# Stick-breaking attention on one core: TensorE turns the logarithm of the weights, ScalarE exponentiates out of PSUM

## The chip, the cores and the metric

One core of a Trainium2 chip runs the whole program. The metric is the device time of one execution in microseconds (us). The kernel before took 1975.42 us, the median of 3 runs (1974.12 to 1976.77).

## The reference

One inference step of a decoder layer: RMSNorm and one wide projection; dilated attention of 12 heads and stick-breaking attention of 8 heads, for 1024 prompt tokens and 8 sampled tokens; sigmoid gates and output projections; a hierarchical mixture of 32 experts; a gated per-layer embedding; a last RMSNorm. The change lies in the stick-breaking attention of the prompt:

```python
z = einsum('bqhd,bkhd->bhqk', q, k) * hd ** -0.5 + bias
log_1mb = where(causal, -softplus(z), 0.0)
suffix  = cumsum(log_1mb, axis=3, reverse=True)
log_a   = -softplus(-z) + suffix - log_1mb
a = where(causal, exp(log_a), 0.0)
out = einsum('bhqk,bkhd->bqhd', a, v)
```

## The kernel before

The program is a row of stages, each written as one instruction list for each engine. The stage of the change is `stick_and_gates`. It does two things side by side: the stick-breaking attention of the prompt, and 10 chunks of the gate projection, whose 344-column matmuls (L666) are dealt out evenly over the steps of the attention, about 11 for each step.

The attention works on 64 units. A unit is one head and one block of 128 queries; heads come in 4 pairs (a pass each), and the 8 query blocks of a pass come in the order 7, 0, 6, 1, 5, 2, 4, 3, so a unit is 8, 1, 7, 2, 6, 3, 5 or 4 tiles of 128 keys wide. Both heads of a block share a pair of steps, an even one and an odd one. Position 0 is the block of 8 tiles, position 1 that of one tile, and so on.

Each engine runs through the same steps s, and each kind of work lags by a fixed number of steps. In step s:

- TensorE issues the scores of both heads, half a block (up to 512 keys) for each step (L630); in odd steps the products with the values (`values`, L650) of the pair whose turning ended in step s-1; half of the step's gate matmuls; the turning of unit s-5 (`turn`, L638: a 128x128 transpose for each tile, in groups of up to four tiles, one PSUM bank for each group, two banks in turn); the other half of the gate matmuls.
- ScalarE first casts a gate weight where one is due (L688) and, in even steps, copies out a finished output block (L709), then scales the scores out of PSUM into z (L718), computes exp(-|z|) and ln(1 + that) of unit s-2 in w (L724, L726), the exponential of unit s-4 in place in z (L731, "RISE"), and copies finished gate sums out of PSUM (L697).
- VectorE adds the causal mask for unit s-1 (L763), runs the reversed running sum for unit s-3 (L769, a scan), splits |z| and max(z, 0) for unit s-1 (L777, L779), subtracts the sum from z for unit s-3 (L784: the logarithm of the weights), and last copies the turned tiles of unit s-5 from PSUM to aT (L791).

`values` waits for `tp_read`, which is counted up by each of those copies: in an odd step it needs the copies of the step before. `turn` waits for the exponential (`a_full`) and for the earlier reader of its PSUM bank (`tp_read`). The lags are set in one line:

```python
FOLD, EXP, SCAN, RISE, TURN, VALUES, EVICT = 1, 2, 3, 4, 5, 6, 7
```

Queues are in order: an engine that waits holds up all that stands behind in its own list. The score bank S of each head is single; z has seven slots, w three, aT two (one for each head).

Of the kernel before, what the change touches and what calls it, by code (L numbers as in the profile page):

```python
# [16 lines left out]
ACT = mybir.ActivationFunctionType  # L17
AX = mybir.AxisListType.X

P = 128  # L20
# [40 lines left out]
def need(eng, sem, value):  # L61

    if not isinstance(value, int) or value > 0:
        eng.wait_ge(sem, value)
# [386 lines left out]
def turn_groups(n):  # L451

    return [(a, min(4, n - a)) for a in range(0, n, 4)]
# [41 lines left out]
def stick_and_gates(nc, g, c0):  # L495
# [5 lines left out]
    with ctx:  # L501
# [5 lines left out]
        STEPS = PAIRS * QT  # L507
        U = 2 * STEPS
        ZB, WB, HALF = 7, 3, 512
        FOLD, EXP, SCAN, RISE, TURN, VALUES, EVICT = 1, 2, 3, 4, 5, 6, 7  # L510
        LAST = U + EVICT
        CH = 2 * KD - c0
        M = KD * 3
# [17 lines left out]
        O = [ps(f"s_O{j}", [P, 512]) for j in range(2)]  # L531
        acc = [ps(f"s_g_acc{j}", [P, 512]) for j in range(2)]
        const, kept = sem("s_const"), g["kept"]
        s_full, z_full, masked, r_full, w_full, e_full, t_full, cum_full, al_full, a_full = map(sem, (
            "s_s_full", "s_z_full", "s_masked", "s_r_full", "s_w_full", "s_e_full", "s_t_full",
            "s_cum_full", "s_al_full", "s_a_full"))
        tp_full, tp_read, o_full, o_read = map(sem, ("s_tp_full", "s_tp_read", "s_o_full", "s_o_read"))
        qkv_in = g["opening"]["qkv_in"]
        gw_in = g["opening"]["gw_in"]
# [8 lines left out]
        def unit(u):  # L548

            st = u // 2  # L550
            return st // QT, u % 2, ORDER[st % QT]
# [15 lines left out]
        def live(s, lag):  # L567

            return 0 <= s - lag < U
# [50 lines left out]
        @block.tensor  # L620
        def _(pe):
            def scores(st, c):
                p_, i = st // QT, ORDER[st % QT]
                x, n = p_ % 2, piece(st, c)
                if st % QT == 0:
                    pe.wait_ge(qkv_in[x], 64 * (p_ // 2 + 1))
                for b in range(2):
                    h = slice(b * HD, (b + 1) * HD)
                    need(pe, z_full, z_first[st, c] - 1 + b)
                    pe.matmul(S[:, b, 0:n], q[x][h, i * P:(i + 1) * P], k[x][h, c * HALF:c * HALF + n],  # L630
                              start=True, stop=True).then_inc(s_full, 1)

            def turn(u):
                pe.wait_ge(a_full, u + 1)
                for n, (t0, m) in enumerate(turn_groups(unit(u)[2] + 1)):
                    need(pe, tp_read, first[u] + n - 1)
                    for t in range(m):
                        last = pe.transpose(tp[(first[u] + n) % 2][:, t * P:(t + 1) * P],  # L638
                                            z[:, u % ZB, (t0 + t) * P:(t0 + t + 1) * P], ident[:, :])
                    last.then_inc(tp_full, 1)  # L640

            def values(st):
                p_, i = st // QT, ORDER[st % QT]
                u = 2 * st + 1
                pe.wait_ge(tp_read, first[u] + count[u])
                need(pe, o_read, st - 1)
                for t in range(i + 1):
                    for b in range(2):
                        h = slice(b * HD, (b + 1) * HD)
                        last = pe.matmul(O[st % 2][h, 0:P], v[p_ % 2][:, t, h], aT[:, b, t * P:(t + 1) * P],  # L650
                                         start=(t == 0), stop=(t == i), skip_group_check=True)
                last.then_inc(o_full, 1)

            def gates(m0, m1):

                for m in range(m0, m1):
                    grp, x = divmod(m, M)
                    c, s = divmod(grp, NSPLIT)
                    t = slice(s * NS, (s + 1) * NS)
                    if x == 0:  # L660
                        pe.wait_ge(gwl_full, c + 1)
                        need(pe, gate_full, grp - 1)
                    kk, part = divmod(x, 3)
                    lhs = (gwl, gwh, gwh)[part]
                    rhs = (uh, ul, uh)[part]
                    last = pe.matmul(acc[grp % 2][:, 0:NS], lhs[:, c % 2, kk, :], rhs[:, kk, t], start=(x == 0),  # L666
                                     stop=(x == M - 1), skip_group_check=True)
                    if x == M - 1:
                        last.then_inc(acc_full, 1)

            for s in range(LAST + 1):
                if s < U and piece(s // 2, s % 2) > 0:
                    scores(s // 2, s % 2)
                if live(s, VALUES) and (s - VALUES) % 2:
                    values((s - VALUES) // 2)
                if s < LAST:
                    gates(fills[s], half(s))
                if live(s, TURN):
                    turn(s - TURN)
                if s < LAST:  # L680
                    gates(half(s), fills[s + 1])

        @block.scalar
        def _(act):
            def cut(c):
                act.wait_ge(gw_in, 16 * (c + 1))
                need(act, acc_full, (c - 1) * NSPLIT)
                act.activation(gwh[:, c % 2, :, :], gw[:, :, :], ACT.Copy).then_inc(gwh_full, 1)  # L688

            def evict(grp):  # L690
                c, s = divmod(grp, NSPLIT)
                if s == 0 and c < 2:
                    act.wait_ge(g["decode_out"][c], 16 * ((c0 + 1 - c) // 2))
                if s == 0:
                    need(act, g_out[c % 2], 16 * (c // 2))
                act.wait_ge(acc_full, grp + 1)
                act.activation(gate[:, c % 2, s * NS:(s + 1) * NS], acc[grp % 2][:, 0:NS], ACT.Copy).then_inc(gate_full, 1)  # L697

            cut(0)
            act.preload_act_table_set("natural_log_exp_and_others")  # L700
            for s in range(LAST + 1):
                for c in range(1, CH):
                    if cut_at[c] == s:
                        cut(c)
                if live(s, EVICT) and (s - EVICT) % 2:
                    st = (s - EVICT) // 2
                    p_, i = st // QT, ORDER[st % QT]
                    act.wait_ge(o_full, st + 1)
                    act.activation(obT[:, p_, i * P:(i + 1) * P], O[st % 2][:, 0:P], ACT.Copy).then_inc(o_read, 1)  # L709
                if s < U and piece(s // 2, s % 2) > 0:  # L710
                    st, c = divmod(s, 2)
                    n = piece(st, c)
                    for b in range(2):
                        u = 2 * st + b
                        act.wait_ge(s_full, z_first[st, c] + b + 1)
                        if c == 0 and u >= ZB:
                            act.wait_ge(tp_full, first[u - ZB] + count[u - ZB])
                        act.activation(z[:, u % ZB, c * HALF:c * HALF + n], S[:, b, 0:n], ACT.Identity, scale=SCALE,  # L718
                                       bias=bias[st // QT % 2][:, b:b + 1]).then_inc(z_full, 1)
                if live(s, EXP):  # L720
                    u = s - EXP
                    n = (unit(u)[2] + 1) * P
                    act.wait_ge(w_full, u + 1)
                    act.activation(w[:, u % WB, 0:n], w[:, u % WB, 0:n], ACT.Exp, scale=-1.0).then_inc(e_full, 1)  # L724
                    act.wait_ge(e_full, u + 1)
                    act.activation(w[:, u % WB, 0:n], w[:, u % WB, 0:n], ACT.Ln, bias=1.0).then_inc(t_full, 1)  # L726
                if live(s, RISE):
                    u = s - RISE
                    n = (unit(u)[2] + 1) * P
                    act.wait_ge(al_full, u + 1)  # L730
                    act.activation(z[:, u % ZB, 0:n], z[:, u % ZB, 0:n], ACT.Exp).then_inc(a_full, 1)  # L731
                for grp in range(CH * NSPLIT):
                    if evict_at[grp] == s:
                        evict(grp)
# [11 lines left out]
        def _(dve):  # L746
# [5 lines left out]
            for s in range(LAST + 1):  # L752
# [27 lines left out]
                if live(s, SCAN):  # L780
# [2 lines left out]
                    dve.wait_ge(cum_full, u + 1)  # L783
                    dve.tensor_tensor(z[:, u % ZB, 0:n], z[:, u % ZB, 0:n], w[:, u % WB, 0:n],  # L784
                                      ALU.subtract).then_inc(al_full, 1)
                if live(s, TURN):
                    u = s - TURN
                    need(dve, o_full, u // 2)
                    for n, (t0, m) in enumerate(turn_groups(unit(u)[2] + 1)):
                        dve.wait_ge(tp_full, first[u] + n + 1)  # L790
                        dve.tensor_copy(aT[:, u % 2, t0 * P:(t0 + m) * P],  # L791
                                        tp[(first[u] + n) % 2][:, 0:m * P]).then_inc(tp_read, 1)


def dilated(nc, g):
# [2196 lines left out]
```

## Time and profile before

| what | value |
|---|---|
| median of 3 runs | 1975.42 us |
| profiled execution, span | 1976.0 us |
| stage of the change, about | 508 to 797 us of the span |
| TensorE / VectorE / ScalarE busy over the span | 88% / 61% / 49% |

The page gives for each engine its busy time over the whole span; a stage has to be read by itself. For that there are views of a stretch: busy time of each engine in a window with the granted TensorE clock (1.00 is 2.4 GHz, 0.50 is 1.2 GHz, values between are means), waits by who waited for whom, groups of instructions by line, and instructions in order of time. A matmul's row shows its latency, so rows of following matmuls overlap; the busy time of a window is their union.

### The profile page before, as it was taken

The numbers are of one execution on the slowest core, as the hardware profiler recorded it, in microseconds if no ns is written. First come the engines' busy times: TensorE is split into PE (matmuls) and PEld (weight loads), VectorE is DVE, ScalarE is ACT, GpSimd is POOL, SyncE is SP. The second block draws the span as 40 slices with busy tenths as digits, with TensorE's granted clock in tenths as the row PEclk, the third lists the DMA queues.
The fourth block names the chain that finished last, engine by engine and source line by source line (L and its number), as shares of the span: only waits on it lengthen the run. The fifth ranks groups of instructions, "written<-read, shape, count | busy, mean of one in ns | idle before, by whom it ended". The sixth has DMA issues, their size and how long they took to land. (4 is left out here: it accounts for less than half of the span.)

```text
span 1976.0 us, 27569 instructions
## 1 busy us (share of the span) xinstructions
PE 1747.3 (88%) x9832; PEld 1483.3 (75%) x9832; DVE 1199.8 (61%) x1550; ACT 976.7 (49%) x1392; POOL 213.4 (11%) x316
## 2 busy tenths in 40 slices
PE   5999999989888888798549967999999999997497
PEld 4999999978666666576548845788888888885485
DVE  6111222153589998442473355899999999996485
ACT  4121111111476776155342014778777877785255
POOL 1000111120000000300130012111111111110100
PEclk8999999989999999899779978999999999999699
DMA  5343455453351200612454316999999999994641
GB/s 170 107 135 110 128 177 159 126 193 118 102 183 54 76 22 23 203 50 76 170 200 153 118 66 238 390 372 379 372 383 379 372 382 381 384 370 189 225 150 66
DMA packets 156394, 392.77 MB, mean 199 GB/s; under 512 B 21923, under 2 KB 95251, under 8 KB 135828
## 3 DMA queue, kind: packets, MB, share of 16 engines
q1 hardware_dynamic: 120676, 320.28, 45.4%
q0 software_dynamic: 15424, 36.00, 5.7%
q10 hardware_dynamic: 20208, 35.35, 5.0%
q8 instruction: 54, 0.88, 0.2%
q14 instruction: 32, 0.26, 0.0%
HBM read 335.32 MB, written 80.58 MB: 210 GB/s over the span
## 5 line engine op out<-in xcount | busy, mean ns | idle before, releaser
L97 PE MATMUL p_acc<-uh,p_wl 128*128 128x344 f32 x720 | 234.3, 325 | 9.6 <-DVE ul L415 9.6
L98 PE MATMUL p_acc<-ul,p_wh 128*128 128x344 f32 x720 | 230.7, 320 | 0.0
L99 PE MATMUL p_acc<-uh,p_wh 128*128 128x344 f32 x720 | 230.5, 320 | 0.0
L392 ACT ACTIVATE p_zc<-p_acc 128x344 f32<-128x344 f32 x90 | 41.2, 458 | 290.2 <-PE p_acc L99 286.4
L2543 DVE TENSOR_TENSOR x_wgl<-x_wg,x_wgh 128x2048 fp32r<-128x2048 f32 x66 | 148.3, 2288 | 36.1 <-ACT x_wgh L2480 20.0
L2543 DVE TENSOR_TENSOR x_wul<-x_wu,x_wuh 128x2048 fp32r<-128x2048 f32 x66 | 148.3, 2289 | 18.7 <-ACT x_wuh L2480 18.7
L2565 DVE TENSOR_TENSOR x_wdl<-u,x_wdh 128x1024 fp32r<-128x1024 f32 x128 | 148.2, 1220 | 10.3 <-ACT x_wdh L2486 10.3
L97 PEld LDWEIGHTS p_acc<-uh,p_wl 128*128 128x128 f32 x720 | 135.9, 189 | 13.1 <-issue 8.6
L428 DVE COPY u<-p_tp 128x512 f32<-128x512 f32 x40 | 25.8, 686 | 185.2 <-PE p_tp L345 185.1
L98 PEld LDWEIGHTS p_acc<-ul,p_wh 128*128 128x128 f32 x720 | 136.0, 189 | 0.0
L99 PEld LDWEIGHTS p_acc<-uh,p_wh 128*128 128x128 f32 x720 | 135.8, 189 | 0.0
L2486 ACT ACTIVATE x_wdh<-u 128x1024 fp32r<-128x1024 f32 x128 | 124.8, 1059 | 0.0
L2480 ACT ACTIVATE x_wgh<-x_wg 128x2048 fp32r<-128x2048 f32 x64 | 119.0, 1915 | 0.0
L2480 ACT ACTIVATE x_wuh<-x_wu 128x2048 fp32r<-128x2048 f32 x64 | 118.6, 1906 | 0.0
L97 PE MATMUL x_G<-x_wgh,x_xl 128*128 128x512 f32 x256 | 102.9, 402 | 6.1 <-DVE x_xl L2537 6.1
L97 PE MATMUL x_Y<-x_wdh,x_hl 128*128 128x512 f32 x256 | 103.6, 405 | 3.8 <-DVE x_hl L2560 3.8
L97 PE MATMUL x_U<-x_wuh,x_xl 128*128 128x512 f32 x256 | 103.4, 404 | 0.0
L99 PE MATMUL x_G<-x_wgh,x_xh 128*128 128x512 f32 x256 | 102.8, 401 | 0.0
L98 PE MATMUL x_G<-x_wgl,x_xh 128*128 128x512 f32 x256 | 102.3, 400 | 0.0
L99 PE MATMUL x_U<-x_wuh,x_xh 128*128 128x512 f32 x256 | 101.2, 395 | 0.0
L98 PE MATMUL x_U<-x_wul,x_xh 128*128 128x512 f32 x256 | 101.0, 394 | 0.0
L99 PE MATMUL x_Y<-x_wdh,x_hh 128*128 128x512 f32 x256 | 100.8, 394 | 0.0
(383 smaller groups left out, 4269.7 us busy)
## 6 DMA issues: line engine op xcount, KB each, us to landing
x_wg<-in_w_gate SPq DMA_DIRECT2D x64, 1024.0 KB
x_wu<-in_w_up SPq DMA_DIRECT2D x64, 1024.0 KB, 7.7
u<-in_w_down SPq DMA_DIRECT2D x32, 2048.0 KB, 12.2
zT<-p_zc ACTq DMA_DIRECT2D x30, 516.0 KB, 3.5
p_w<-in_w_in SPq DMA_DIRECT2D x30, 512.0 KB, 5.5
ztok<-u POOLq DMA_DIRECT2D x20, 512.0 KB, 4.6
m_gate<-gT SPq DMA_DIRECT2D x16, 516.0 KB, 4.4
f_y<-ys POOLq DMA_DIRECT2D x16, 512.0 KB, 5.1
```

Source lines behind the costliest of these rows:

```text
L97: pe.matmul(out, w_low, m_high, start=first, stop=False)
L98: pe.matmul(out, w_high, m_low, start=False, stop=False)
L99: return pe.matmul(out, w_high, m_high, start=False, stop=last)
L392: act.activation(zc[:, b, s * NS:(s + 1) * NS], acc[b * NSPLIT + s][:, 0:NS], ACT.Copy).then_inc(zc_full, 1)
L428: dve.tensor_copy(zk[:, b, t0:t0 + m, :], tp[n][:, :, :]).then_inc(zk_full, 1)
L2480: act.activation(wh[:, HALVES[half], :], w[:, HALVES[half], :], ACT.Copy).then_inc(full, 1)
L2486: act.activation(wdh[:, k, :], wd[:, b, k, :], ACT.Copy).then_inc(dh_full, 1)
L2543: dve.tensor_tensor(wl[:, s, :], w[:, s, :], wh[:, s, :], ALU.subtract).then_inc(full, 1)
L2565: dve.tensor_tensor(wdl[:, k, :], wd[:, b, k, :], wdh[:, k, :], ALU.subtract).then_inc(dl_full, 1)
```

## The change

The exponential in place (RISE, one instruction for each unit, SBUF to SBUF, at lag 4) goes. TensorE turns the logarithm z itself, so `turn` waits for `al_full` (VectorE's subtraction, lag 3) instead of `a_full`; its lag stays 5. The copies of the turned tiles from PSUM to aT leave VectorE; in their place ScalarE writes aT with an exponential that reads the PSUM tile, one instruction for each group of up to four tiles, at the same lag 5, after the exp and ln of unit s-2 and ahead of the gate copies.

```diff
-        FOLD, EXP, SCAN, RISE, TURN, VALUES, EVICT = 1, 2, 3, 4, 5, 6, 7
+        FOLD, EXP, SCAN, TURN, VALUES, EVICT = 1, 2, 3, 5, 6, 7
@@ tensor
             def turn(u):
-                pe.wait_ge(a_full, u + 1)
+                pe.wait_ge(al_full, u + 1)
@@ scalar
-                if live(s, RISE):
-                    u = s - RISE
-                    n = (unit(u)[2] + 1) * P
-                    act.wait_ge(al_full, u + 1)
-                    act.activation(z[:, u % ZB, 0:n], z[:, u % ZB, 0:n], ACT.Exp).then_inc(a_full, 1)
+                if live(s, TURN):
+                    u = s - TURN
+                    need(act, o_full, u // 2)
+                    for n, (t0, m) in enumerate(turn_groups(unit(u)[2] + 1)):
+                        act.wait_ge(tp_full, first[u] + n + 1)
+                        act.activation(aT[:, u % 2, t0 * P:(t0 + m) * P], tp[(first[u] + n) % 2][:, 0:m * P],
+                                       ACT.Exp).then_inc(tp_read, 1)
@@ vector
-                if live(s, TURN):
-                    u = s - TURN
-                    need(dve, o_full, u // 2)
-                    for n, (t0, m) in enumerate(turn_groups(unit(u)[2] + 1)):
-                        dve.wait_ge(tp_full, first[u] + n + 1)
-                        dve.tensor_copy(aT[:, u % 2, t0 * P:(t0 + m) * P],
-                                        tp[(first[u] + n) % 2][:, 0:m * P]).then_inc(tp_read, 1)
```

## Rows read from the trace of the kernel before

**Rows 1.** The page, part 1: busy time, share of the span, instructions.
```profile
PE 1747.3 (88%) x9832; PEld 1483.3 (75%) x9832; DVE 1199.8 (61%) x1550; ACT 976.7 (49%) x1392; POOL 213.4 (11%) x316
```
**Rows 2.** Busy time by stretch: start:end, length, engines, PEclk, DMA share, GB/s.
```profile
508.00:796.00 288.00, 245.76 (x1739) 194.87 (x1740) 247.43 (x425) 192.86 (x358) 0.00 (x0) 0.95 0.22 70
645.50:713.50 68.00, 59.37 (x431) 45.61 (x432) 63.96 (x110) 49.62 (x93) 0.00 (x0) 0.97 0.22 71
713.50:781.00 67.50, 55.62 (x408) 44.17 (x404) 61.72 (x109) 46.42 (x88) 0.00 (x0) 0.95 0.04 17
781.00:797.00 16.00, 14.69 (x113) 13.32 (x113) 7.72 (x12) 4.29 (x10) 0.00 (x0) 0.89 0.01 2
```
**Rows 3.** Waits of the stage, 508 to 798: total us, times, longest.
```profile
ACT s_z L718 <- PE s_S L630: 59.7, 31, 4.4
PE s_O L650 <- DVE s_aT L791: 39.3, 30, 3.1
```
**Rows 4.** Waits of one pass of eight blocks, 645.5 to 713.5.
```profile
PE s_O L650 <- DVE s_aT L791: 8.6, 8, 2.7
```
**Rows 5.** Groups of the stage by line, shapes together: count, busy, mean ns.
```profile
L718 ACT ACTIVATE s_z<-s_S,s_bias 128x512 f32<-128x512 f32 (+3 forms) x96 | 50.4, 576 | 60.1 <-PE s_S L630 59.7
L791 DVE COPY s_aT<-s_tp 128x512 f32<-128x512 f32 (+3 forms) x96 | 50.2, 550 | 11.7 <-PE s_tp L638 11.7
...
L731 ACT ACTIVATE s_z<-s_z 128x1024 f32<-128x1024 f32 (+7 forms) x64 | 42.8, 668 | 4.6 <-DVE s_z L784 4.6
```
**Rows 6.** Groups of the stage, one shape each: copies and exponentials.
```profile
L791 DVE COPY s_aT<-s_tp 128x512 f32<-128x512 f32 x48 | 32.2, 684 | 9.7 <-PE s_tp L638 9.7
...
L697 ACT ACTIVATE u<-s_g_acc 128x344 f32<-128x344 f32 x30 | 13.3, 443 | 10.9 <-PE s_g_acc L666 10.9
...
L688 ACT ACTIVATE s_g_wh<-u 128x1024 fp32r<-128x1024 f32 x9 | 9.5, 1054 | 13.4 <-DMA u<-in_w_in 7.3 <-PE s_g_acc L666 6.1
...
L709 ACT ACTIVATE u<-s_O 128x128 f32<-128x128 f32 x32 | 8.5, 266 | 10.1 <-PE s_O L650 10.0
```
**Rows 7.** Timeline, position 1 of a pass: start, us, engine, line, idle before.
```profile
653.46 0.49 PE L630 MATMUL s_S<-u 64*128 64x128 f32 x4
...
653.98 0.63 ACT L718 ACTIVATE s_z<-s_S,s_bias 128x128 f32<-128x128 f32 x2 [0.75 <-PE s_S L630]
...
655.58 1.06 ACT L726 ACTIVATE s_w<-s_w 128x1024 f32<-128x1024 f32 x1
...
656.55 0.61 ACT L731 ACTIVATE s_z<-s_z 128x512 f32<-128x512 f32 x1
...
658.25 0.88 DVE L791 COPY s_aT<-s_tp 128x512 f32<-128x512 f32 x2
...
659.18 1.09 PE L650 MATMUL s_O<-s_aT,u 128*64 128x128 f32 x14 [2.75 <-DVE s_aT L791]
```
**Rows 8.** Timeline, position 3 of the same pass.
```profile
672.20 0.70 PE L630 MATMUL s_S<-u 64*128 64x256 f32 x4
...
674.65 0.95 ACT L726 ACTIVATE s_w<-s_w 128x896 f32<-128x896 f32 x1
...
675.78 0.44 PE L650 MATMUL s_O<-s_aT,u 128*64 128x128 f32 x4 [0.21 <-DVE s_aT L791]
```
**Rows 9.** Timeline, position 4 of the same pass.
```profile
679.40 1.13 PE L630 MATMUL s_S<-u 64*128 64x512 f32 x4
...
682.17 0.42 ACT L726 ACTIVATE s_w<-s_w 128x256 f32<-128x256 f32 x1
...
684.50 0.28 DVE L791 COPY s_aT<-s_tp 128x128 f32<-128x128 f32 x1
...
684.84 0.44 PE L650 MATMUL s_O<-s_aT,u 128*64 128x128 f32 x4 [1.94 <-DVE s_aT L791]
```
**Rows 10.** Busy time and clock of 3 us at and after position 1's wait.
```profile
658.00:661.00 3.00, 1.82 (x21) 1.49 (x21) 3.00 (x5) 2.07 (x4) 0.00 (x0) 0.82 0.00 0
661.00:664.00 3.00, 3.00 (x13) 2.77 (x13) 2.71 (x6) 0.24 (x1) 0.00 (x0) 0.61 0.00 0
```

More of the change, by code:

```diff
@@ L533, in stick_and_gates @@
         const, kept = sem("s_const"), g["kept"]
-        s_full, z_full, masked, r_full, w_full, e_full, t_full, cum_full, al_full, a_full = map(sem, (
+        s_full, z_full, masked, r_full, w_full, e_full, t_full, cum_full, al_full = map(sem, (
             "s_s_full", "s_z_full", "s_masked", "s_r_full", "s_w_full", "s_e_full", "s_t_full",
-            "s_cum_full", "s_al_full", "s_a_full"))
+            "s_cum_full", "s_al_full"))
         tp_full, tp_read, o_full, o_read = map(sem, ("s_tp_full", "s_tp_read", "s_o_full", "s_o_read"))
```

## The prediction

> **What bounds the kernel now.** I read the page first [rows 1]: TensorE leads over the whole span, which says nothing of this stage. The busy time by stretch [rows 2] says it: in the 288 us of the stage VectorE is busy 247.4, TensorE 245.8, ScalarE 192.9; in the two passes shown VectorE has 63.96 of 68.0 and 61.72 of 67.5 us, 91 to 94%, TensorE 82 to 87%. Third the waits [rows 3]: TensorE stands still for 39.3 us, 30 times, ahead of the products with the values, each time for VectorE's copy into aT; that is nearly all of its idle time (288 − 245.8 = 42.2). ScalarE waits 59.7 us for scores, so it has room. So VectorE's list sets the pace, and TensorE feels it at one place: the copy that stands last in VectorE's step.
>
> The order of time shows how. At position 1 [rows 7] TensorE arrives at the value products at 659.18 − 2.75 = 656.43 and waits until the copies end at 658.25 + 0.88 = 659.13, though ScalarE had everything but its last exponential done at 656.6.
>
> **The change part by part.** *VectorE* loses 96 copies, 50.2 us [rows 5]: 247.4 becomes 197, or 68% of the stage. What was left of its list has a step of slack: exp and ln of a unit come one step after its split, the scan one step after the ln, the turn two steps after the subtraction. I cost VectorE at nothing afterwards; were that cover gone, ScalarE's exp would wait for up to a step of VectorE, 197 / 64 = 3.1 us, each time.
>
> *ScalarE* loses 64 exponentials, 42.8 us [rows 5], and gains 96 that read PSUM. No row shows this one. Nearest are the two copies from PSUM without a bias operand [rows 6]: 344 columns in 443 ns, 128 in 266 ns, so 0.82 ns a column, and 581, 476, 371 and 266 ns for 512, 384, 256 and 128 columns. The group counts are those of the copies, 48, 16, 16 and 16: 48 x 0.581 + 16 x (0.476 + 0.371 + 0.266) = 45.7 us. The upper bound is L718, the same shapes and counts out of PSUM with a bias operand, 50.4 us; the lower one is no change at all, 42.8. I take 45.7, since the two copies have the same operands. So ScalarE goes from 192.9 to about 196 us, at most 201: not a bound by sum.
>
> The Trainium skill (Perfetto Trace Analysis, Optimizing Scalar/DVE Operations) advises fewer, larger operations and puts ScalarE's fixed cost at about 93 ns from SBUF and 51 ns from PSUM. It speaks against 96 in place of 64, but by its figures the fixed part would be 96 x 0.051 − 64 x 0.093, an estimate of −1.1 us against the +2.9 above; either is small beside the waits.
>
> *TensorE* does the same work. `turn` waits for a result that is a step older, so it waits no longer there. What changes is who releases the value products: ScalarE's new exponential, last but for the gate copies in an in-order list. It needs the transposes of its own step, which stand mid-step on TensorE, and it comes after that step's scores, exp and ln. Behind it wait the gate copy and the next step's scores. So I take the even steps one at a time, from the scores' start, which stays the origin since ScalarE waits there now.
>
> Position 1 [rows 7]: the slot at which RISE starts, 656.55, is where the new exponential starts (TensorE's transposes of that step were over before). Five tiles, a group of four and one of one: 0.581 + 0.266 less an overlap of 0.09 (consecutive rows of ScalarE overlap by that: ln ends 656.64, RISE starts 656.55) = 0.76. Ready at 657.3, against TensorE's 656.43: wait 0.95 to 1.1, now 2.75. Position 3 [rows 8]: ln ends 675.60, eight tiles take 2 x 0.581 − 0.09 = 1.07, ready at 676.6; TensorE arrives at 675.78 − 0.21 = 675.57: wait 1.1, now 0.21, so a loss of 0.9. Position 4 [rows 9]: ln ends 682.6, one tile 0.27, ready at 682.8; TensorE arrives at 684.84 − 1.94 = 682.90: no wait, now 1.94. The rest goes the same way: in positions 1, 3, 5 and 7 ScalarE's exp and ln are of a long block (8 to 5 tiles) and so is the turned one, and I get 1.1 to 1.2 us of wait each; in positions 0, 2, 4 and 6 they are short beside TensorE's scores, and I get 0, 0, 0 and 0.35. A pass waits 4 x 1.1 + 0.35, about 4.8 us. Now it waits 8.6 in one pass [rows 4] and 39.3 / 4 = 9.8 on average [rows 3]. Saved: 39.3 − 4 x 4.8 = 20.
>
> Two corrections. ScalarE casts a gate weight 9 times, 1.05 us each [rows 6]. Where it falls into the idle time ahead of the scores it costs nothing now; with the new exponential ending later in odd steps that idle time shrinks, so I charge about 0.7 us for half of them, with some for late gate copies: −3 us. And the clock: through the wait at position 1 the granted clock is 0.82, and in the 3 us behind it 0.61, nearly the 1.2 GHz level, with TensorE busy throughout [rows 10]; the stage has a mean of 0.95, so half speed costs 0.05 x 288 = 14 us at most. Shorter long waits may spare some. The stage's last 16 us, with 14.69 busy, have only 1.3 to give [rows 2]. I credit 1 us for both, keep up to 10 for the range, and nothing below zero beyond rival C.
>
> The Trainium skill (Perfetto Trace Analysis, Matmul Optimizations) says that the matmul engine's power follows its utilisation, so matmuls should run back to back. By that the longest waits cost twice, and shortening them should give most of those 14 us; this trace agrees in that the clock is down behind the 2.75 us wait.
>
> *Sum*: 20 − 3 + 1 = 18 us. The profiled span of 1976.0 lies 0.6 above the median of the runs, so nothing has to be added around it; I subtract from the median: 1975.4 − 18 = **1957.4**. With ScalarE's dearer bound the eight-tile exponential costs 0.2 more and the long positions give back 16 x 0.15, 2 to 3 us.
>
> **Rivals.**
> *A, full cover.* ScalarE is always ready in time, the waits go to about zero, part of the clock comes back: 39.3 and a few more, 1933. For it: ScalarE has 95 us of idle time. Against: that idle time lies ahead of the scores, not ahead of the exponential. Chance 0.09.
> *B, the wait changes its name.* VectorE is relieved but the value products wait as long for ScalarE, since exp and ln of a long block start later than I read them (scores late, cast in between). Position 3 already loses. Gain 0 to 5, about 1973. Chance 0.16.
> *C, slower.* TensorE and ScalarE run in lockstep: the new exponential holds back the next scores' copy, the single score bank holds TensorE at its scores, and each long position waits twice. It decides against the change when the mean wait of the 32 value products passes 39.3 / 32 = 1.23 us; at 1.6 us, which is my long-position figure plus half a microsecond at every position, the stage loses 12 us, and more half-clock stretches add some: 1988. For it: new waits are spread over every long position. Against: ScalarE's sum is far from the stage's length. Chance 0.13.
> *D, a dear exponential* (at the 50.4 us bound, or above it) is no case of its own: it moves the forecast by 3 us, or into B.
>
> **How the numbers follow.** Forecast 0.62, own range 1945 to 1968. A 0.09, B 0.16, C 0.13. The range runs from 1940, the forecast with the whole clock term, to 1974, B with little gain; it leaves out C and most of A, 0.19. A measurement of this kernel tells 0.2%, 4 us, from no change. Faster: 0.62 + 0.09 + a quarter of B = 0.75. Same: the rest of B, 0.12. Slower: 0.13.
>
> **What would show it.** In the profile after: VectorE at about 197 us in the stage; ScalarE near 196 to 201; the stage some 18 us shorter; TensorE waiting about 20 us for ScalarE's aT, at positions 1, 3, 5 and 7, about 1.1 us each, and hardly at the even ones; ScalarE's wait for scores down; the new exponential of 512 columns at 0.58 us; the first half-clock stretch of each pass shorter. Wrong if the wait for aT is over 30 us (B), if TensorE's scores wait for ScalarE's z (C), or if ScalarE's exp waits for VectorE's split (no slack after all).

## The result, and the profile after

The changed kernel takes 1944.59 us (median of 4 runs, 1943.36 to 1945.50), beside 1976.1 us (1974.12 to 1977.58) for the kernel before in the same comparison: a ratio of 0.9844, interval 0.9830 to 0.9858, or 31.5 us less. The forecast was 18 us less, to 1957.4. The whole range, 1940 to 1974, held the time; the forecast's own, 1945 to 1968, missed it by 0.4 us, at the end where half-clock stretches go away. The profiled execution has a span of 1942.6 us, 33.4 less than that of before.

First the page, and the stage as a whole. I bound the stage at both ends by the same instructions in each kernel: ScalarE's table load ahead of it and GpSimd's first instruction of the next stage. The columns are those of [rows 2].

```profile
PE 1732.4 (89%) x9832; PEld 1470.9 (76%) x9832; DVE 1153.7 (59%) x1454; ACT 978.4 (50%) x1424; POOL 213.6 (11%) x316
```

The stage in the kernel before, then in the changed one:

```profile
499.35:798.89 299.54, 251.46 (x1774) 199.92 (x1772) 248.65 (x426) 194.65 (x360) 0.00 (x0) 0.95 0.23 75
```
```profile
498.22:763.35 265.13, 239.15 (x1774) 190.36 (x1772) 203.28 (x330) 196.52 (x392) 0.00 (x0) 0.99 0.26 85
```

The stage is 34.4 us shorter; the stages ahead of it are 1.1 shorter and those behind it 2.1 longer, within the scatter of the runs. So the gain is here. VectorE is down by 45.4 us, ScalarE up by 1.9. (The 96 copies had rows of 50.2 us in sum; rows of consecutive instructions overlap, so the engine's busy time falls by less. The forecast took off the whole 50.2.) And TensorE, which issues the same 1774 matmuls, is busy 12.3 us less, at a mean clock of 0.99 instead of 0.95.

The waits of the changed stage, answering to [rows 3]:

```profile
ACT s_aT L732 <- PE s_tp L638: 24.8, 26, 2.8
ACT s_z L718 <- PE s_S L630: 23.8, 34, 2.6
PE s_O L650 <- ACT s_aT L732: 18.8, 20, 1.2
...
DVE s_z L765 <- ACT s_z L718: 6.2, 5, 2.1
```

The value products now wait 18.8 us, 20 times, never over 1.2 us; before it was 39.3 us, 30 times, up to 3.1. That is 20.5 us of the 34.4. With the 12.3 us less busy time 32.8 are accounted for; 1.6 us are other small idle times of TensorE.

The new exponential by shape, answering to [rows 6]:

```profile
L732 ACT ACTIVATE s_aT<-s_tp 128x512 f32<-128x512 f32 x48 | 27.4, 588 | 11.2 <-PE s_tp L638 11.1
L732 ACT ACTIVATE s_aT<-s_tp 128x384 f32<-128x384 f32 x16 | 7.7, 482 | 5.1 <-PE s_tp L638 5.1
L732 ACT ACTIVATE s_aT<-s_tp 128x256 f32<-128x256 f32 x16 | 6.0, 376 | 4.3 <-PE s_tp L638 4.3
L732 ACT ACTIVATE s_aT<-s_tp 128x128 f32<-128x128 f32 x16 | 4.3, 269 | 4.3 <-PE s_tp L638 4.3
```

588, 482, 376 and 269 ns, where the prediction had 581, 476, 371 and 266 from its two copies.

Position 1 in the order of time, answering to [rows 7]:

```profile
636.18 0.49 PE L630 MATMUL s_S<-u 64*128 64x128 f32 x4
...
636.70 0.63 ACT L718 ACTIVATE s_z<-s_S,s_bias 128x128 f32<-128x128 f32 x2
637.22 1.06 ACT L724 ACTIVATE s_w<-s_w 128x1024 f32<-128x1024 f32 x1
637.50 0.71 PE L638 MATMUL s_tp<-ident,s_z 128*128 128x128 f32 x5
638.31 1.06 ACT L726 ACTIVATE s_w<-s_w 128x1024 f32<-128x1024 f32 x1
639.27 0.75 ACT L732 ACTIVATE s_aT<-s_tp 128x512 f32<-128x512 f32 x2
639.90 0.46 ACT L697 ACTIVATE u<-s_g_acc 128x344 f32<-128x344 f32 x1
640.07 1.20 PE L650 MATMUL s_O<-s_aT,u 128*64 128x128 f32 x17 [1.08 <-ACT s_aT L732]
```

The transposes end at 638.21, but exp and ln of the block of 8 tiles hold ScalarE until 639.37. The turned exponential, 0.75 us, releases the value products after a wait of 1.08, where it was 2.75. Positions 3 and 4, answering to [rows 8, 9]:

```profile
654.14 1.07 ACT L732 ACTIVATE s_aT<-s_tp 128x512 f32<-128x512 f32 x2
...
655.26 0.99 PE L650 MATMUL s_O<-s_aT,u 128*64 128x128 f32 x14 [1.06 <-ACT s_aT L732]
...
661.99 0.26 ACT L732 ACTIVATE s_aT<-s_tp 128x128 f32<-128x128 f32 x1
662.31 0.44 PE L650 MATMUL s_O<-s_aT,u 128*64 128x128 f32 x4
```

Position 3 waits 1.06 us (0.21 before) and position 4 not at all (1.94 before).

The clock at and after position 1's wait, answering to [rows 10]:

```profile
639.00:642.00 3.00, 1.93 (x24) 1.76 (x25) 2.87 (x6) 2.97 (x6) 0.00 (x0) 1.00 0.00 0
642.00:645.00 3.00, 3.00 (x18) 2.01 (x17) 2.87 (x4) 1.65 (x4) 0.00 (x0) 1.00 0.00 0
```

Read microsecond by microsecond through both stages, the kernel before has a stretch of about 7 us at clock 0.50 at the stage's opening, and in its body seven of about 3.4 us. Each of the seven begins within 2 us of the end of a wait of the value products, of 2.00, 2.08, 1.77, 2.75, 2.55, 3.10 and 2.17 us. Not each long wait has one: behind the one of 2.69 us the clock stays at 1.00 for 9 us, up to the next wait, of 1.77, which does. The wait of 2.69 us and the clock 3 us after it, then the clock behind the wait of 1.77:

```profile
592.53 1.31 PE L650 MATMUL s_O<-s_aT,u 128*64 128x128 f32 x20 [2.69 <-DVE s_aT L791]
...
595.35:596.35 1.00, 1.00 (x7) 0.72 (x7) 1.00 (x2) 0.00 (x0) 0.00 (x0) 1.00 0.00 0
...
602.35:603.35 1.00, 1.00 (x14) 0.95 (x10) 0.94 (x2) 0.58 (x2) 0.00 (x0) 0.50 0.00 0
```

The changed kernel has the stretch at the opening alone. Seven times 3.4 us at half speed are 12 us.

### The profile page after: what moved, and what is told of

Same layout as the page of the kernel before. It is cut to its first block and busy times, and to the rows that moved or that the text cites. A ratio compares the mean times of both kernels' runs of the same rounds, so it can differ in the third digit from the quotient of the medians.

```text
span 1942.6 us, 27505 instructions
## 1 busy us (share of the span) xinstructions
PE 1732.4 (89%) x9832; PEld 1470.9 (76%) x9832; DVE 1153.7 (59%) x1454; ACT 978.4 (50%) x1424; POOL 213.6 (11%) x316
## 5 line engine op out<-in xcount | busy, mean ns | idle before, releaser
L97 PE MATMUL p_acc<-uh,p_wl 128*128 128x344 f32 x720 | 234.1, 325 | 10.2 <-DVE ul L415 10.2
## 6 DMA issues: line engine op xcount, KB each, us to landing
u<-in_w_down SPq DMA_DIRECT2D x32, 2048.0 KB, 12.1
```

The costliest lines, as they stand in the source:

```text
L97: pe.matmul(out, w_low, m_high, start=first, stop=False)
```

## The experiments

All times are medians beside the kernel before on the same chip (1973.5 us in the first four, 1973.8 in the last four; the gain is taken against that). The changed kernel was not run again beside them, so where a run is compared with it, its gain is set against the 31.5 us above, or its stage against the 265.1 us. The profile of the kernel before is of a run of 1975.4 us, some 2 us above these medians, so differences from its stage of 299.5 come out larger than the gains. My theory after the result had two parts: *L*, VectorE's load and the place of its copy made the value products wait, and what is left of the wait is ScalarE's order; *C*, waits of 2 to 3 us were paid for twice, by half-clock stretches behind them.

### Copies to ScalarE, exponential left in place

```diff
 kernel before:
                     act.activation(z[...], z[...], ACT.Exp).then_inc(a_full, 1)      # RISE stays
+                if live(s, TURN):                                                     # moved from VectorE
+                        act.wait_ge(tp_full, first[u] + n + 1)
+                        act.activation(aT[...], tp[...][:, 0:m * P], ACT.Copy).then_inc(tp_read, 1)
```

> One part of the change alone: the copies from PSUM move from VectorE to ScalarE, while the exponential stays in place in SBUF at lag 4 (64 more ScalarE instructions, 42.8 us, than the changed kernel). Theory V (VectorE's relief is the gain, but the value products wait for whatever stands ahead of the copy in ScalarE's step): each even step has 0.4 to 1.0 us more ahead of the copy, and ScalarE's load is 196 + 43 = 239 us of a stage that was 265; the wait for aT grows from 18.8 to 30 to 45 us, and the long waits bring half-clock stretches back; 1960 to 1973. Rival M (only the load taken off VectorE counts, the merging of two instructions into one is a detail): 1945 to 1950.

Measured: 1966.89 us, ratio 0.9968 (0.9957 to 0.9979), a gain of 6.6 us. Its stage and its wait:

```profile
498.05:786.79 288.74, 245.87 (x1774) 195.84 (x1772) 204.19 (x330) 230.58 (x456) 0.00 (x0) 0.96 0.25 78
...
PE s_O L650 <- ACT s_aT L737: 35.7, 30, 2.2
```

VectorE has the changed kernel's load, 204 us, and most of the gain is not there. The wait is 35.7 us and four half-clock stretches are back in the body of the stage. Wait and time lie where theory V had them, and rival M (1945 to 1950) is out: the load off VectorE is not the gain by itself. Beside the changed kernel the stage is 23.6 us longer, 16.9 of it in the wait for aT and 6.7 in TensorE's busy time, with those four stretches. So in this order of ScalarE's list the merging matters. The run does not tell two things apart: the copy stands behind one more instruction, and ScalarE has 34 us more to do (230.6 against 196.5). With the copy ahead of exp and ln it was not tried.

### VectorE's old load put back

```diff
 changed kernel, vector:
+                if live(s, TURN):
+                    for n, (t0, m) in enumerate(turn_groups(unit(u)[2] + 1)):
+                        dve.wait_ge(filled, 1 + first[u] + n)
+                        dve.tensor_tensor(fill[:, 0:m * P], fill[:, 0:m * P], fill[:, 0:m * P],
+                                          ALU.subtract).then_inc(filled, 1)
```

> The changed kernel with VectorE's old load put back: one subtraction on a scratch tile for each group of turned tiles, of the same width and duration as the old copy (0.69 us for 512 columns), at the end of VectorE's step as before, but nothing waits for it. Theory L (VectorE's load set the pace): VectorE is at 203 + 50 = 253 us again, its step is as long as before, and the stage goes back toward 285 to 295 us; 1962 to 1976. Rival P (the place mattered: the copy was the last thing of VectorE's step and the value products hung on it; the load itself is under the stage's length): scan and split come later but have a step of slack; stage 265 to 275, 1945 to 1955.

Measured: 1963.57 us, 0.9949 (0.9931 to 0.9967), a gain of 9.9 us. The filler took 553 ns on average; the copy had taken 550.

```profile
500.59:783.85 283.26, 245.91 (x1774) 195.77 (x1772) 250.32 (x427) 198.16 (x392) 0.00 (x0) 0.96 0.25 79
...
ACT s_w L725 <- DVE s_w L780: 30.1, 33, 2.4
...
PE s_O L651 <- ACT s_aT L733: 29.9, 21, 2.8
```

Theory L holds, with a time in its range and a stage a little short of it (285 to 295 us): with VectorE at 250 us again the stage goes from 265 to 283, 11.1 us of the 18.1 in the wait for aT and 6.8 in TensorE's busy time, with four half-clock stretches in the body. Rival P (265 to 275 us, time 1945 to 1955) is out. The load shows in a place where the changed kernel has 1.0 us: ScalarE's exp waits 30.1 us for VectorE's split, and the turned exponential stands behind that exp. How the gain divides depends on the measure. By the medians 9.9 us of the 31.5 remain with the load put back, so 21.6 need the lighter load; by the stages 16.3 of 34.4 remain and 18.1 need it (the profiled execution of this run is 4 us above its median, and 5 us longer than the changed kernel outside the stage). So half to two thirds of the gain need VectorE's lighter load. The rest comes with the value products no longer hanging on the end of VectorE's step; that part is argued from what is left, not tested by itself.

### Four long stalls, and the same total in twelve short ones

```diff
 changed kernel, scalar, ahead of the turned exponential:
+                    if s % (2 * QT) == 2:                     # position 1 of each pass
+                        for x in range(3):
+                            act.wait_ge(filled, 1 + 3 * (s // (2 * QT) - 1) + x)
+                            act.activation(fill[:, :], fill[:, :], ACT.Copy).then_inc(filled, 1)
```

The second kernel has one such copy in steps with s % 16 in (2, 6, 10) instead: 12 in all, as in the first.

> The changed kernel with three 512-column copies on a scratch tile ahead of ScalarE's turned exponential at position 1 of each pass, 4 places, about 1.85 us each, 7.4 us in all: the wait for aT there grows from 1.1 to about 2.9 us, as long as it was before the change. Theory C (a wait of nearly 3 us is paid twice, since a half-clock stretch of 3.4 us follows, 1.7 us each): plus 12 to 15 us, 1957 to 1960, with two to four stretches of clock 0.5 behind position 1. Rival N (the clock's recovery is not due to the shorter waits): plus at most 7.4 us, 1952 or less, clock as in the changed kernel.

> The same total of stalls, 12 copies of 512 columns on a scratch tile, but one at a time, at positions 1, 3 and 5: the waits there grow from 1.1 to about 1.7 us. Theory C: no wait is near 3 us, the clock stays at 1.00 through the body of the stage, and the cost is the stalls alone, plus 5 to 7.5 us, 1950 to 1952. Rival N or a rival by which the sum of waits decides over the clock: as dear as the long stalls, within 2 us of that run.

Measured: long stalls 1956.81 us (0.9921, 0.9903 to 0.9939), short stalls 1948.06 us (0.9870, 0.9850 to 0.9891). Stage and wait of the long ones, and the 6 us around position 1:

```profile
498.27:775.36 277.09, 244.72 (x1774) 195.40 (x1772) 203.57 (x330) 202.99 (x404) 0.02 (x2) 0.96 0.25 81
641.00:644.00 3.00, 1.27 (x10) 0.98 (x8) 2.87 (x6) 2.90 (x5) 0.00 (x0) 1.00 0.00 0
644.00:647.00 3.00, 1.81 (x18) 1.81 (x20) 2.88 (x3) 2.97 (x6) 0.00 (x0) 0.64 0.00 0
...
PE s_O L651 <- ACT s_aT L737: 25.1, 21, 3.1
```

The same of the short ones:

```profile
499.66:768.85 269.19, 240.39 (x1774) 192.23 (x1772) 203.39 (x330) 202.22 (x404) 0.01 (x1) 0.98 0.26 83
...
PE s_O L651 <- ACT s_aT L737: 24.4, 20, 1.7
```

By their gains, 16.7 and 25.5 us, the two are 14.8 and 6.0 us above the changed kernel; theory C had 12 to 15 and 5 to 7.5. (Both times are a little under the ranges of the expectations; the kernel before was also 2.6 us faster on this chip.) Rival N, at most 7.4 for the long stalls, is out.

The waits sum to nearly the same, 25.1 and 24.4 us. Three of the four long stalls show as waits, of 3.08, 2.93 and 2.93 us; the fourth falls in the drain, behind the last scores, where no wait for aT is over 0.9. Behind the first two of the waits lies a half-clock stretch of 3.4 us each, and one of about 7 us begins within the third. By the medians the long stalls cost 8.8 us more than the short ones, by the stages 7.9 (277.1 against 269.2). Of that 4.3 us are TensorE's busy time: behind position 1 the clock is 0.64 again. A further 2.8 us lie at the stage's opening, where neither edit acts: there TensorE waits 4.2 us for ScalarE's copy of the scores in the profile of the long stalls, with the opening's half-clock stretch behind that wait, and 1.4 us in that of the short ones, with the stretch ahead of it. Which of the two an execution gets is not explained by the edits, and what the executions without a profile had is not known. Sampled by the microsecond, (1 − clock) summed over the stage is 10.2 us with the long stalls, 5.1 with the short ones and 3.4 in the changed kernel. Theory C holds: the same sum of waits is dearer in long ones, and 4.3 us of that is shown to be the clock. Its short case missed in one detail: the stalls show as eleven waits of 1.58 to 1.75 us, and one of them, 1.74 us long, did bring a half-clock stretch, while four others of 1.74 and 1.75 did not.

### Value products behind half the gate matmuls

```diff
 tensor, kernel before and changed kernel:
-                if live(s, VALUES) and (s - VALUES) % 2:
-                    values((s - VALUES) // 2)
                 if s < LAST:
                     gates(fills[s], half(s))
+                if live(s, VALUES) and (s - VALUES) % 2:
+                    values((s - VALUES) // 2)
```

> The kernel before with one thing moved on TensorE: in odd steps the value products come after the first half of the step's gate matmuls, so about 0.85 us of work stands where TensorE waited for VectorE's copy. Theory L (VectorE's load sets the pace of the kernel before, the 39.3 us wait is where that shows): VectorE keeps 249 us in a stage of 299 and the wait turns up elsewhere; gain 3 to 12 us, part of it from shorter long waits and fewer half-clock stretches; 1963 to 1971. Rival W (the wait is a latency that any work can cover): 30 waits x 0.85 = 25 us less, 1950 or below.

> The same move in the changed kernel, whose waits for aT are 20 of about 0.95 us (18.8). Theory L (no engine's load is at the stage's length any more, the waits are latency): most is covered, 13 to 17 us less than the changed kernel, 1928 to 1934. Rival S (ScalarE would be late by as much elsewhere, since its turned exponential waits for TensorE's transposes too): under 5 us less, 1940 or more.

Measured: in the kernel before 1962.21 us (0.9943, 0.9925 to 0.9961), in the changed one 1932.20 us (0.9806, 0.9776 to 0.9836). Waits for aT, first of the kernel before with the move, then of the changed kernel with it:

```profile
PE s_O L650 <- DVE s_aT L791: 29.3, 25, 2.6
```
```profile
PE s_O L650 <- ACT s_aT L732: 6.7, 15, 0.6
```

The stage of the kernel before with the move:

```profile
498.04:782.75 284.71, 249.13 (x1774) 196.05 (x1772) 247.63 (x426) 195.01 (x360) 0.00 (x0) 0.96 0.25 79
```

The same move covers 12.1 of 18.8 us of wait in the changed kernel, but only 10.0 of 39.3 in the kernel before, though 30 waits with 0.85 us of work each would have made 25. VectorE still had 247.6 us in a stage of 284.7, and part of what was hidden at one value product came back at others. In the kernel before the gain of 11.6 us is in theory L's range, with two half-clock stretches fewer in the stage's body; rival W (1950 or below) is out. In the changed kernel the time is in L's range, but the saving is not: 10.1 us by the gains and 11.6 by the stages, where 13 to 17 were expected. One of its four runs, 1941.6, lies far from the others, and its interval just touches that of the changed kernel (0.9830 to 0.9858), so here the trace is the better evidence. Set side by side, the two runs separate a wait that is a load from a wait that is a latency.

### ScalarE's order turned around in even steps

```diff
 changed kernel, scalar:
+                if s % 2:
+                    logs()                  # exp and ln of unit s-2, odd steps
                 if live(s, TURN):
                     ...                     # the turned exponential
+                if s % 2 == 0:
+                    logs()                  # even steps: behind it
```

> The changed kernel with ScalarE's order turned around in even steps: the turned exponential ahead of the exp and ln of unit s-2. My theory of the wait (the value products wait since exp and ln of a long block stand ahead in ScalarE's list): ScalarE is then ready about 1 to 2 us earlier, the wait for aT falls from 18.8 to under 4 us, scans come later but have a step of slack; stage 247 to 253, 1928 to 1934. Rival T (the wait is set by the transposes of the same step): the wait stays over 12 us, and the time within 4 us of the changed kernel.

> Both moves in the changed kernel. Each covers the same 18.8 us, so together little more than one of them: stage 245 to 250, 1926 to 1932, unless the gap between TensorE's odd-step work and ScalarE's lets more go. Rival: the two disturb each other (value products later, so output blocks and aT's slots later), slower than the better of the two by over 3 us.

Measured: 1923.50 us (0.9743, 0.9725 to 0.9761), and with the value products moved as well 1924.42 us (0.9754, 0.9735 to 0.9773). Stage and waits of the first:

```profile
498.05:744.56 246.51, 238.47 (x1774) 190.14 (x1772) 202.52 (x330) 195.19 (x392) 0.00 (x1) 0.99 0.28 91
...
ACT s_w L725 <- DVE s_w L785: 8.0, 7, 2.2
```

The wait for aT falls from 18.8 us to 0.5, once; TensorE is busy 238.5 us of 246.5, and 4.2 of the rest is the wait at the opening. ScalarE's exp now waits 8.0 us for the split, all inside its slack. So the left-over wait was the order of ScalarE's list, not its load and not the transposes. Time and stage came out below what I had expected, 1928 to 1934 and 247 to 253 us: the wait went entirely, and not only to under 4 us. The second move has nothing left to hide: the two times are within each other's intervals. The turned order is the best version here, with or without it, 50 us under the kernel before and some 19 under the changed kernel.

## Why the prediction was right, and what it undersized

The direction, the bound and the waits were right; the size was not: 31.5 us came where 18 were forecast. Nearly all of the shortfall is two of the sum's terms.

**The bound.** VectorE's load set the pace: shown by the filler and by the move of the value products in the kernel before. The reading of the last copy in the step as the releaser was right too: with the load put back but the place changed, 10 us remain by the medians and 16 by the stages. VectorE was forecast at 197 us in the stage and measured 203.3. In the same bounds the kernel before had 248.7, and 248.7 − 50.2 is 198.5; the other 4.8 us are the overlap of rows told above. The forecast's sum does not use VectorE's load, so this moved nothing.

**ScalarE's price.** 45.7 us from two copies' rows; the four groups sum to 45.4, or 2.6 more than the 42.8 of the exponentials in place; ScalarE's busy time rose by 1.9. The estimate of −1.1 us, worked out from the fixed costs in the Trainium skill (Perfetto Trace Analysis, Optimizing Scalar/DVE Operations), is not borne out; the rows of the copies were the better source.

**TensorE's wait, position by position.** Forecast 0.95 to 1.1, 1.1 and 0 us at positions 1, 3 and 4; measured 1.08, 1.06 and 0. At position 1 the prediction's own subtraction, 657.3 − 656.43, gives 0.87, so its 0.95 to 1.1 came from no row. In the first half of the stage the long waits are 1.2 us, in the second 1.06 to 1.09. A pass was to wait 4.8 us; 18.8 / 4 = 4.7. Saved: 20 forecast, 20.5 measured. The premise held: ScalarE still waited for the scores, 34 times, 23.8 us in all.

**The charge of 3 us for casts and late gate copies** was not paid. The casts still fitted into ScalarE's idle time: behind those at 569.69 and 628.92 it waited another 0.18 and 0.17 us for the scores. The waits at the value products show no trace of them: 1.06 and 1.08 us ahead of and behind the cast at 658.77.

**The clock** is the term that was undersized: 1 us credited for clock and tail together, up to 10 kept for the range, 12.3 measured in TensorE's busy time. The step that failed is "shorter long waits may spare some". The rows held what was needed: the product 0.05 x 288 = 14 us stood in the text, 3.4 of it belongs to the opening, and the rest lies behind waits of 1.8 to 3.1 us, nearly all of which the forecast itself had cut to 1.1. The kernel before had waits of 1.0 to 1.4 us too, and none of them with a stretch behind it. By its own waits the forecast should have credited nearly all. Its range says that 1940 is "the forecast with the whole clock term"; 1957.4 less the 13 us not yet credited is 1944.4, which is what was measured. The tail was read too low as well: it holds one of the seven stretches, so it had 1.7 us beside its idle 1.3. The Trainium skill's sentence (Perfetto Trace Analysis, Matmul Optimizations) that matmuls should run back to back since the engine's power follows utilisation pointed that way, and the runs agree as far as they go: 0.64 behind a wait of 2.9 us, 1.00 behind one of 1.08.

With both terms mended the sum is 20.5 + 12, or 32.5 us, against 34.4 in the stage and 31.5 between the medians. Both terms erred to the same side, so the shortfall is their sum; that the measured time still lies in the whole range is due to the wide end kept for the clock.

**The rivals.** Full cover did not occur in the changed kernel, but was reached by one more change of order. The wait did change its name, at half its length. The lockstep did not: TensorE's scores waited for ScalarE's copy once, at the opening, as before.

## What to carry to other kernels

When an engine waits at one place, ask whether the wait is a load or a latency: put some of its own work in front of it, and see whether the wait shrinks by that much or comes back further on. Relieving the loaded engine shows its worth only if the work lands at a place in the other engine's list where the next reader does not wait behind unrelated work; here a merged instruction gave 31 us, the same copies unmerged 7, and the merged instruction ahead of exp and ln instead of behind them another 19. And where TensorE's clock is below 1.00 behind waits that a change shortens, count the half-speed stretches one by one and credit those whose wait goes.

## What the hardware showed that was not expected

TensorE's waits ahead of the value products, over all ten traces, set beside the half-clock stretches behind them: each of the eight waits of 2.73 us or more has a stretch, and none up to 1.47 us has. In between it went either way. Waits of 1.49, 1.74, 1.77 and 2.64 us had one; others of 1.78, 1.94, 2.11, 2.30 and 2.69 us did not. The length of one wait does not decide it in that range, and what does stays open. A stretch took 1.7 us from TensorE; one of the waits of 2.93 us came with a stretch of about 7 us, which took 3.4.

Waits of nearly the same sum cost 8.8 us more by the medians in the run with long ones. 4.3 us of it is TensorE's busy time at the lower clock; of the rest, 2.8 us lie at the opening of the stage in the profiled executions, where no stall was put.
